# Order of work around three waits of TensorE in a hybrid state-space, attention and expert layer: scores, routing and bias moved

## The chip, the cores and the metric

The kernel runs on one NeuronCore of a Trainium2 chip. The metric is the device time of one execution in microseconds (us), less is better. Engines are named as the profile names them: PE is TensorE (PEld its weight loads, PEq its instruction queue), DVE is VectorE, ACT is ScalarE, POOL is GpSimd, SP is the engine that here only issues transfers. PE works on arrays of SBUF (on-chip memory, 128 partitions) and writes PSUM, eight banks of 512 f32 columns.

## The reference

One layer on 1024 tokens of 1024 channels, all in f32:

```python
h = rmsnorm(x, norm_mix_g); proj = h @ w_in                 # q, k, v (512 each), 8 gates, u (512)
attn = forgetting_attention(q, k, v, log_f)                 # 8 heads of 64
ssm = s5_mixer(u, ...)                                      # 32 groups of 16 channels, state 64
mixed = concatenate([rmsnorm(attn, attn_out_g), rmsnorm(ssm, ssm_out_g)])
x = x + mixed @ w_out
h = rmsnorm(x, norm_ffn_g)
top_val, top_idx = lax.top_k(h @ w_router + b_router, 4)    # of 32 experts
gates = softmax(top_val)
x = x + sum_k gates[k] * (clamped_swiglu(h @ w_gu[e] + b_gu[e]) @ w_dn[e] + b_dn[e])
x = x + ple_in * sigmoid(rmsnorm(x, norm_ple_g) @ w_ple_gate)   # ple_in = p @ w_ple_proj
out = rmsnorm(x, norm_final_g)
```

## The kernel before, in words

Each engine has its own hand-written program, in order; semaphores join them. A wait holds everything that stands behind it on its engine. PSUM banks are dealt out by hand. An f32 matmul is two instructions of PE ("x8" for four of them). The stages in order of time:

1. **Projection and state space (0 to 289 us).** PE computes the 34 units of `PROJ` into banks 2 to 5. Behind every second unit of v, k and q stands a piece of the state-space mixer (`PIECE_AFTER`, `piece`); the last, `piece("out", 3)`, stands behind the last q unit and writes banks 0 and 1, which ACT copies to `u`.
2. **Attention (290 to 417 us).** 32 tiles (a pair of heads, a block of 128 queries). `scores(s)` on PE, `row_low(s)` on DVE, `exp(s)` on ACT, `recip(s)` on DVE, a scaling on POOL, `turn_probs` and `values` on PE. `scores` runs `AHEAD` = 3 tiles ahead, in banks 0 to 3. POOL's loop first waits for the last piece's copy and does the first part of a gelu beside the attention.
3. **Gate of the state-space output (417 to 450 us)**: `wglu` matmuls; DVE and ACT make `ssmT` from them.
4. **Output projection and routing (452 to 602 us).** `project(t, n)` is eight matmuls of 512 columns, four from `attnT`, four from `ssmT`, into banks 0, 1 or 2, 3 in turn. `row_squares` sums squares into banks 4 to 7. DVE (`resid`) adds the result to `x1`, DVE and ACT normalise the block (`norm_rows`, `ffn_norm`), `turn_rows(t)` transposes it, ACT copies it, `route(t)` computes the router's logits, and DVE (`logits`) the four best.
5. **Bias and tables (602 to 656 us).** DVE works out where each (token, expert) row goes: `ohr` and `ohc`, in four parts; ACT scales a part (`tokens_in`), PE multiplies it (L1765), DVE takes `rowid` from the sum, and POOL gathers the first rows of the experts by it. DVE then makes `passtab`, which goes over memory to `passrow`; engines load numbers of passes from it. Beside that, POOL spreads the gates (`gsp`, L575), PE turns them (L1741), and `bias(un)`, un = 0 to 15, adds gate times `b_dn` to `x1`: a matmul of 32 rows (L1754) and an identity matmul that adds `x1` itself (L1755), then a copy by ACT (`bias_out`, L801). SP's first four chunks of the first expert's weights `wg` are issued in this stage, the other four and the four of `wd` once `passrow` and the rows are there.
6. **Experts (656 to 2233 us).** One pass per expert, by number of rows: six narrow passes (L1865, L1887), then wider ones (L1808, L1825). Each pass loads 12 chunks of 1 MB; a chunk's transfer is issued when PE has freed its place.
7. **Tail (2233 to 2397 us)**: `pp` matmuls (L1932), gather of expert rows by POOL, `combine` and `finish` on DVE, gate matmuls (L1948).

## Time and profile before

| | us |
|---|---|
| median of 3 runs | 2413.66 |
| the three runs | 2397.08, 2413.66, 2414.1 |
| the profiled execution | 2398.55 |
| its span, first to last instruction | 2397.0 |
| TensorE clock granted, mean over the span | 0.994 of 2.4 GHz |

Times in the rows below are from the start of the span. In a row of the timeline "xN" counts instructions that the view merged, the number in brackets is idle time of the engine before them and who ended it.

### The profile page before, as it was taken

To read this page: it belongs to the slowest core of one execution; us is meant where nothing else is said; L and a number is where in the kernel's file an instruction comes from. 1 tells how busy PE (TensorE), PEld (TensorE's weight loads), DVE (VectorE), ACT (ScalarE), POOL (GpSimd) and SP (SyncE) were. 2 spreads that over 40 slices of the span, in tenths; PEclk is the share of its full clock that TensorE was granted. 3 is DMA by queue.
4 is the path that set the end of the run, shared out by engine and by line. 5 is a ranking of instruction groups with operands and counts; after the bars stand their busy time and mean duration, and the time that the engine had idled before them with its cause. 6 is when DMAs were issued, how large, how long until landed. Compare 5 with 4: busy or idle time off the path is not lost.

```text
span 2397.0 us, 41448 instructions
## 1 busy us (share of the span) xinstructions
PE 2337.4 (98%) x15586; PEld 1634.8 (68%) x15587; DVE 866.1 (36%) x2024; ACT 468.5 (20%) x940; POOL 444.8 (19%) x713
## 2 busy tenths in 40 slices
PE   8999999899899999999999999999999999999998
PEld 5545466455355577888878878878888887767443
DVE  4544476233543342332323323222322222112374
ACT  3110165311211211111111111111111101110244
POOL 0555587000111111011011110101111000000320
PEclk9999999999999999999999999999999999999999
DMA  5100110201499999989889888867777666542550
GB/s 190 41 23 6 40 37 27 126 36 44 170 383 394 390 403 325 317 312 318 316 317 321 311 317 324 299 246 303 305 310 291 243 230 228 211 167 79 210 176 35
DMA packets 94494, 528.58 MB, mean 221 GB/s; under 512 B 17159, under 2 KB 18199, under 8 KB 42335
## 3 DMA queue, kind: packets, MB, share of 16 engines
q1 hardware_dynamic: 72383, 460.19, 51.5%
q0 software_dynamic: 22048, 67.53, 8.1%
q8 instruction: 42, 0.69, 0.1%
q14 instruction: 21, 0.17, 0.0%
HBM read 495.26 MB, written 31.23 MB: 220 GB/s over the span
## 4 chain that ended last, share of the span: by engine, by line
PE 89%; DVE 4%; issue 3%; ACT 3%; DMA 1%; SPq 0%; POOL 0%; ACTq 0%; DVEq 0%
PE ps L1808 37%; PE ps L1825 15%; PE ps L1865 5%; PE ps L1583 5%; PE ps L1887 3%; PE ps L1688 2%; PE ps L1574 2%; PE ps L1690 2%; PE ps L1842 2%; DVE x L1439 2%; PE ps L1778 1%; PE ps L1602 1%; PE ps L1634 1%; PE ps L1620 1%; PE ps L1669 1%
## 5 line engine op out<-in xcount | busy, mean ns | idle before, releaser
L1808 PEld LDWEIGHTS ps<-xT,wg 128*128 128x128 f32 x6912 | 873.0, 191 | 26.6 <-issue 13.5
L1808 PE MATMUL ps<-xT,wg 128*128 128x128 f32 (+3 forms) x6912 | 889.1, 291 | 0.0
L1430 DVE TENSOR_SCALAR gb<-ps,bcur 128x256 f32<-128x256 f32 x216 | 104.5, 484 | 920.5 <-PE ps L1808 920.5
L1825 PE MATMUL ps<-wd,actT 128*128 128x512 f32 x864 | 375.6, 592 | 0.0
L1825 PEld LDWEIGHTS ps<-wd,actT 128*128 128x128 f32 x864 | 162.1, 190 | 193.7 <-issue 187.3
L893 ACT ACTIVATE sg<-gb 128x256 f32<-128x256 f32 x216 | 90.1, 417 | 785.8 <-DVE gb L1430 785.8
L1865 PE MATMUL ps<-wg,xT 128*32 128x256 f32 x2304 | 131.8, 385 | 3.5 <-issue 3.5
L1948 PE MATMUL ps<-wpg,xnT 128*128 128x512 f32 x256 | 112.9, 595 | 6.2 <-ACT xnT L906 6.2
L843 ACT ACTIVATE yb<-ps 128x512 f32<-128x512 f32 x54 | 31.2, 596 | 402.9 <-PE ps L1825 181.4
L1865 PEld LDWEIGHTS ps<-wg,xT 128*32 128x32 f32 x2304 | 73.8, 111 | 53.0 <-issue 6.7
L610 POOL COPY rowc<-rowid 128x2 uint32 (+1 forms) x34 | 8.8, 260 | 518.5 <-PE ps L1778 490.8
L1420 DVE TENSOR_TENSOR tb<-gb,sg 128x256 f32<-128x256 f32 x216 | 91.9, 426 | 34.8 <-ACT sg L893 34.8
L1431 DVE TENSOR_SCALAR ub<-ps,bcur 128x256 f32<-128x256 f32 x216 | 102.5, 475 | 0.0
L628 POOL DMA_DIRECT2D bin__177<-in_b_exp x33 | 19.0, 576 | 420.2 <-issue 292.5
L1423 DVE SCALAR_TENSOR_TENSOR actT<-ub,tb 128x256 f32<-128x256 f32 x216 | 91.8, 425 | 7.4
L1948 PEld LDWEIGHTS ps<-wpg,xnT 128*128 128x128 f32 x256 | 47.5, 190 | 65.9 <-issue 54.5
L641 POOL DMA_DIRECT2D expert_rows<-yb x48 | 35.1, 741 | 236.4 <-ACT yb L850 163.4
L1887 PE MATMUL ps<-wd,actT 128*32 128x256 f32 x1152 | 64.6, 380 | 3.4 <-ACT actT L869 3.4
L645 POOL DMA_DIRECT2D expert_rows<-yb x60 | 30.0, 501 | 188.0 <-ACT yb L843 181.9
L1688 PE MATMUL ps<-wout,attnT 128*128 128x512 f32 x128 | 59.4, 608 | 5.4 <-issue 2.8
L1401 DVE TENSOR_TENSOR gb<-ps,bb 64x256 f32<-64x256 f32 x36 | 15.0, 417 | 122.7 <-PE ps L1865 122.7
L1439 DVE SCALAR_TENSOR_TENSOR x<-yg,gates,x 128x1024 f32<-128x1024 f32 x32 | 41.1, 1284 | 46.7 <-DMA yg<-expert_rows,slots 45.9
(403 smaller groups left out, 2455.1 us busy)
## 6 DMA issues: line engine op xcount, KB each, us to landing
wg<-in_w_gu SPq DMA_DIRECT2D x264, 1024.0 KB, 7.1
wd<-in_w_dn SPq DMA_DIRECT2D x132, 1024.0 KB, 7.3
expert_rows<-yb POOLq DMA_DIRECT2D x48, 256.0 KB, 8.4
expert_rows<-yb POOLq DMA_DIRECT2D x60, 128.0 KB, 4.4
hT<-in_x_cm SPq DMA_DIRECT2D x8, 512.0 KB, 7.2
cumb<-gate_sums SPq DMA_DIRECT2D x4, 1024.0 KB, 4.6
x<-in_x_tm SPq DMA_DIRECT2D x1, 4096.0 KB, 13.5
wout<-in_w_out SPq DMA_DIRECT2D x1, 4096.0 KB, 20.9
```

What stands on the lines that cost most here:

```text
L893: a.activation(sg[:, f % 2, :], gb[:, f % 2, :], ACT.Sigmoid, scale=1.702).then_inc(S("sig_ready"), 1)
L1420: v.tensor_tensor(tb[:, f % 2, :], gb[:, f % 2, :], sg[:, f % 2, :], ALU.mult).then_inc(S("tb_ready"), 1)
L1423: v.scalar_tensor_tensor(actT[:, f, :], ub[:, f % 2, :], -6.0, tb[:, f % 2, :], ALU.max, ALU.mult).then_inc(S("act_ready"), 1)
L1430: v.tensor_scalar(gb[:, f % 2, :], ps[:, f % 2, 0:W], bcur[:, f:f + 1], 7.0, ALU.add, ALU.min).then_inc(S("g_ready"), 1)
L1431: v.tensor_scalar(ub[:, f % 2, :], ps[:, f % 2, W:2 * W], bcur[:, 8 + f:9 + f], 8.0, ALU.add, ALU.min).then_inc(S("gu_evac"), 1)
L1583: ins = m.matmul(ps[:, bank, :], w_[:, k, un[1] * P:un[1] * P + P], hT[:, k, 512 * un[2]:512 * un[2] + 512], start=(k == 0), stop=(k == KT ...
L1688: m.matmul(ps[:, 2 * (w % 2), :], attnT[:, k, t * P:t * P + P], wout[:, k, n * 512:n * 512 + 512], start=(k == 0), stop=(k == 3))
L1808: ins = m.matmul(ps[:, f % 2, g_ * W:g_ * W + w], wg[:, f, k, g_, :], xT[:, k, 0:w], start=(k == 0), stop=(k == KT - 1))
L1825: ins = m.matmul(ps[:, 2 + c, :], actT[:, f, 0:P], wd[:, c, f, :], start=(f == 0), stop=(f == FT - 1))
L1865: ins = m.matmul(ps[GR * j:GR * j + GR, ut % 2, 0:256], xT[:, k, GR * r:GR * r + GR], wg[:, f0:f0 + 2, k, j // 2, :], start=(k == 0), stop ...
L1887: ins = m.matmul(ps[GR * j:GR * j + GR, 2 + r // 2, 256 * (r % 2):256 * (r % 2) + 256], actT[:, f, GR * r:GR * r + GR], wd[:, j // 2, f, 2 ...
L1948: ins = m.matmul(ps[:, 2 + n, :], xnT[:, t % 2, k, :], wpg[:, k, n * 512:n * 512 + 512], start=(k == 0), stop=(k == KT - 1))
```

## The change

Four things are done; no arithmetic is added or left out except that a quarter of the bias no longer passes through an identity matmul.

- **Scores first.** PE computes `scores(0)` and `scores(1)` right behind the last q unit, then `piece("out", 3)`, which now writes banks 6 and 7. ACT does `exp(0)` ahead of the piece's copy. `scores(0)` waits only for the q units before the last.
- **Projection split.** `attn_part(0, 0)`, `attn_part(0, 1)` stand ahead of the wait for `ssmT`. `row_squares` writes bank 7 alone, so both projections of block 1 stand right behind it, the first in banks 4 and 5. `turn_rows(t)` stands behind `project(t + 1, 1)` and `route(t)` one block later than before.
- **Bias in quarters.** `bias(r, ...)`: four 32-row matmuls in a row, in four different row strips and four banks, then four identity matmuls. Quarters 0 and 1 stand ahead of the table matmuls, quarter 2 behind them, quarter 3 behind the expert passes, in banks 0, 1, 6, 7 and without identity matmuls: DVE adds it to `x1` with two instructions. ACT copies quarters 0 to 2.
- **Work off POOL.** `gsp` is now 32 small ACT instructions (16 for each half of the tokens, the second half between `tokens_in`), the two memsets go to DVE behind `passtab`.
- The first `turn_half` of the experts' rows waits no longer for `passrow`, the second rows and the last bias copy.

```diff
+OUT_BANK = [0] * (NB - 1) + [6]
+WO_BANK = [0, 2, 4] + [2 * (w % 2) for w in range(3, 16)]
...
-            pool.wait_ge(S("rt_evac"), 9)
-            pool.wait_ge(S("sel_ready"), 8)
             pool.wait_ge(S("hs_st"), 16 * 8)
-            g.tensor_tensor(gsp[:, :, :, :], oh[:, :, :, :].rearrange("p t k e -> p k t e"),
-                            gates[:, :, :].rearrange("p t k -> p k t").unsqueeze(3).to_broadcast([P, TOPK, 8, 32]), ALU.mult).then_inc(S("gs_ready"), 1)
-            link(g.memset(yb[:, 1, :], 0.0))
-            g.memset(xT[:, :, P:W], 0.0).then_inc(S("gu_evac"), 2)
...
-            for s in range(AHEAD):
+            exp(0)
+            piece("out", NB - 1)
+            for s in range(1, AHEAD):
                 exp(s)
...
+            act.wait_ge(S("rt_evac"), 9)
+            act.wait_ge(S("hs_st"), 16 * 8)
+
+            def gates_in(half, part):
+                t = 4 * half + part
+                for k in range(TOPK):
+                    ins = a.activation(gsp[:, k, t, :], oh[:, t, k, :], ACT.Copy, scale=gates[:, t, k:k + 1])
+                if part == 3:
+                    ins.then_inc(S("gs_ready"), 1)
...
+            def bias_out(r):
+                for j in range(4):
+                    act.wait_ge(S("wo_mm"), 17 + 4 * r + j)
+                    a.activation(x1[:, 4 * (r // 2) + j, 512 * (r % 2):512 * (r % 2) + 512], ps[:, 2 + j, :], ACT.Copy).then_inc(S("wo_evac"), 1)
...
-            for un in range(6):
-                bias_out(un)
-            tokens_in(0)
-            for q in range(1, 4):
+            for part in range(4):
+                gates_in(0, part)
+            gates_turned(0)
+            bias_out(0)
+            bias_out(1)
+            for q in range(4):
                 tokens_in(q)
-                bias_out(5 + q)
-            for un in range(9, 16):
-                bias_out(un)
+                gates_in(1, q)
+            gates_turned(1)
+            bias_out(2)
...
+            dve.wait_ge(S("hs_st"), 16 * 8)
+            link(v.memset(yb[:, 1, :], 0.0))
+            v.memset(xT[:, :, P:W], 0.0).then_inc(S("gu_evac"), 2)
...
-            dve.wait_ge(S("wo_evac"), 32)
+            dve.wait_ge(S("wo_evac"), 28)
+            dve.wait_ge(S("wo_mm"), 29)
+            v.tensor_tensor(x1[:, 4:6, 512:D], ps[:, 0:2, :], x1[:, 4:6, 512:D], ALU.add)
+            v.tensor_tensor(x1[:, 6:8, 512:D], ps[:, 6:8, :], x1[:, 6:8, 512:D], ALU.add).then_inc(S("wo_evac"), 1)
...
+            pe.wait_ge(S("pj_evac"), len(PROJ) - 2)
+            pe.wait_ge(S("sy_evac"), NB - 1)
+            pe.wait_ge(S("k_evac"), NB)
+            scores(0)
             pe.wait_ge(S("pj_evac"), len(PROJ))
-            pe.wait_ge(S("sy_evac"), NB)
-            for s in range(AHEAD):
+            scores(1)
+            piece("out", NB - 1)
+            for s in range(2, AHEAD):
                 scores(s)
...
             pe.wait_ge(S("an_ready"), 4)
+            pe.wait_ge(S("out_ld"), 48)
+            attn_part(0, 0)
+            attn_part(0, 1)
             pe.wait_ge(S("ssm_ready"), 8)
-            pe.wait_ge(S("out_ld"), 48)
-            project(0, 0)
-            project(0, 1)
+            ssm_part(0, 0)
+            ssm_part(0, 1)
             row_squares()
+            project(1, 0)
+            project(1, 1)
             pe.wait_ge(S("sm_ready"), 1)
-            for t in range(8):
-                if t + 1 < 8:
-                    project(t + 1, 0)
+            turn_rows(0)
+            for t in range(1, 7):
+                project(t + 1, 0)
+                route(t - 1)
+                project(t + 1, 1)
                 turn_rows(t)
-                if t + 1 < 8:
-                    project(t + 1, 1)
-                route(t)
+            route(6)
+            turn_rows(7)
+            route(7)
...
+            def bias(r, banks, alone):
+                i, n = r // 2, r % 2
+                for j in range(4):
+                    ins = m.matmul(ps[:, banks[j], :], gdT[32 * j:32 * j + 32, i, :], bdn[32 * j:32 * j + 32, 512 * n:512 * n + 512],
+                                   start=True, stop=alone, skip_group_check=True)
+                if alone:
+                    ins.then_inc(S("wo_mm"), 1)
+                else:
+                    for j in range(4):
+                        m.matmul(ps[:, banks[j], :], ident, x1[:, 4 * i + j, 512 * n:512 * n + 512], start=False, stop=True,
+                                 skip_group_check=True).then_inc(S("wo_mm"), 1)
+            gates_turn(0)
             pe.wait_ge(S("out_ld"), 112)
...
+            bias(0, (2, 3, 4, 5), False)
+            pe.wait_ge(S("wo_evac"), 20)
+            bias(1, (2, 3, 4, 5), False)
             for q in range(4):
                 pe.wait_ge(S("tok_ready"), 2 * q + 2)
...
+            gates_turn(1)
+            pe.wait_ge(S("wo_evac"), 24)
+            bias(2, (2, 3, 4, 5), False)
...
+            pe.wait_ge(S("rows0_ld"), 16)
+            turn_half(0)
             pe.wait_ge(S("tab_ld"), 16)
-            pe.wait_ge(S("rows0_ld"), 16)
-            pe.wait_ge(S("rows1_ld"), 16)
             n_next = pe.alloc_register("n_rows_next")
             pe.reg_load(n_next, passrow[0:1, 2:3])
-            pe.wait_ge(S("wo_evac"), 32)
-            turn_rows_in(n_next)
+            pe.wait_ge(S("rows1_ld"), 16)
+            pe.wait_ge(S("wo_evac"), 28)
+            turn_second(n_next)
...
+            pe.wait_ge(S("xt_evac"), npass * 2 + 2)
+            bias(3, (0, 1, 6, 7), True)
             pe.wait_ge(S("wpp_ld"), 32)
             pe.wait_ge(S("y_evac"), npass + 1)
             for i in range(16):
+                if i == 2:
+                    pe.wait_ge(S("wo_evac"), 29)
```

**Scores, on PE.** Where stage 1 ends, PE's program was (the last q unit reads `w_q`; `toep` and `xs_r`, `xs_i` are the last state-space piece, `kA,qA` with `mask_qk` are scores):

```order
L1583 MATMUL ps<-hT,w_q 128x512 x16
L1523 MATMUL ps<-toep,ugT 128x128 x8
L1530 MATMUL ps<-ca_r,xs_r 128x128 x8
L1530 MATMUL ps<-ca_i,xs_i 128x128 x8
L1602 MATMUL ps<-kA,qA 128x128 x2
L1606 MATMUL ps<-mask_qk,ident_b 128x128 x2
L1602 MATMUL ps<-kA,qA 128x512 x4
```

and is now:

```order
L1605 MATMUL ps<-hT,w_q 128x512 x16
L1624 MATMUL ps<-kA,qA 128x128 x2
L1628 MATMUL ps<-mask_qk,ident_b 128x128 x2
L1624 MATMUL ps<-kA,qA 128x512 x4
L1628 MATMUL ps<-mask_qk,ident_b 128x128 x2
L1545 MATMUL ps<-toep,ugT 128x128 x8
L1552 MATMUL ps<-ca_r,xs_r 128x128 x8
L1552 MATMUL ps<-ca_i,xs_i 128x128 x8
L1624 MATMUL ps<-kA,qA 128x256 x2
```

The first two tiles' scores stand ahead of the piece, the third's behind it.

**Projection, on PE.** At the start of stage 4 PE's program was (`wout` with `attnT` or `ssmT` is the projection, `ones` the squares, `cst,hn` a block's transposes, `wr` its routing):

```order
L1688 MATMUL ps<-wout,attnT 128x512 x4
L1690 MATMUL ps<-wout,ssmT 128x512 x4
L1688 MATMUL ps<-wout,attnT 128x512 x4
L1690 MATMUL ps<-wout,ssmT 128x512 x4
L1680 MATMUL ps<-ones,sqs 128x128 x8
L1680 MATMUL ps<-ones,sqat 128x128 x8
L1688 MATMUL ps<-wout,attnT 128x512 x4
L1690 MATMUL ps<-wout,ssmT 128x512 x4
L1699 MATMUL ps<-cst,hn 128x128 x8
```

and is now:

```order
L1718 MATMUL ps<-wout,attnT 128x512 x8
L1723 MATMUL ps<-wout,ssmT 128x512 x8
L1710 MATMUL ps<-ones,sqs 128x128 x8
L1710 MATMUL ps<-ones,sqat 128x128 x8
L1718 MATMUL ps<-wout,attnT 128x512 x4
L1723 MATMUL ps<-wout,ssmT 128x512 x4
L1718 MATMUL ps<-wout,attnT 128x512 x4
L1723 MATMUL ps<-wout,ssmT 128x512 x4
L1737 MATMUL ps<-cst,hn 128x128 x8
```

Both `attnT` halves of block 0 stand together and first, and both projections of block 1 stand between the squares and the first transposes.

**Bias, on ACT.** In stage 5, behind the copy of the ranks (`smap`), ACT's program was (`gdT` the turned gates, `x_133` the bias copies into `x1`, `ohc` the tables):

```order
L793 ACTIVATE smap<-ps 128x256
L795 ACTIVATE gdT<-ps 128x256
L801 ACTIVATE x_133<-ps 128x512 x6
L809 ACTIVATE ohc<-ohc,cst 128x432 x4
L801 ACTIVATE x_133<-ps 128x512
L809 ACTIVATE ohc<-ohc,cst 128x432 x2
```

and is now:

```order
L791 ACTIVATE smap<-ps 128x256
L800 ACTIVATE gsp<-oh,gates 128x32 x16
L807 ACTIVATE gdT<-ps 128x128
L813 ACTIVATE x_133<-ps 128x512 x8
L821 ACTIVATE ohc<-ohc,cst 128x432 x2
L800 ACTIVATE gsp<-oh,gates 128x32 x4
L821 ACTIVATE ohc<-ohc,cst 128x432 x2
```

Sixteen spreads of the gates stand ahead of everything else, two more bias copies stand ahead of the first table part, and four spreads behind each table part.

## Rows read from the trace of the kernel before

**Rows 1.** Timeline of projection and routing: start us, us, instruction, [idle before <- who].

```profile
452.48 5.37 PE L1688 MATMUL ps<-wout,attnT 128*128 128x512 f32 x8 [2.82 <-issue]
...
474.34 3.67 PE L1688 MATMUL ps<-wout,attnT 128*128 128x512 f32 x8 [2.62 <-DVE x L1244]
...
505.42 1.95 PE L1709 MATMUL ps<-wr,h2T 128*128 128x128 f32 x16
...
583.96 3.60 PE L1690 MATMUL ps<-wout,ssmT 128*128 128x512 f32 x8
...
592.37 1.42 PE L1699 MATMUL ps<-cst,hn 128*128 128x128 f32 x8 [3.03 <-DVE hn L1253]
...
594.90 3.78 PE L1709 MATMUL ps<-wr,h2T 128*128 128x128 f32 x16 [1.11 <-ACT h2T L784]
...
598.80 0.19 DVE L1257 TENSOR_TENSOR lg<-ps,brt 128x32 f32<-128x32 f32 x1 [4.47 <-PE ps L1709]
```

**Rows 2.** Timeline where attention starts.

```profile
285.27 1.95 PE L1523 MATMUL ps<-toep,ugT 128*128 128x128 f32 x16
...
290.48 0.49 PE L1602 MATMUL ps<-kA,qA 64*128 64x128 f32 x4 [1.28 <-ACT u L693]
...
295.56 0.16 DVE L1168 RECIPROCAL rden<-den 128x2 f32<-128x2 f32 x1
```

**Rows 3.** Timeline at the start of the tail.

```profile
2234.18 27.73 PE L1932 MATMUL ps<-wpp,ppT 128*128 128x512 f32 x64 [1.18 <-ACT yb L845]
```

**Rows 4.** Stretches: us, busy us (instructions) by engine, PE clock granted, DMA share, GB/s.

```profile
586.00:608.00 22.00, 14.25 (x67) 11.37 (x66) 13.28 (x53) 4.66 (x8) 3.81 (x3) 0.77 0.14 48
700.00:840.00 140.00, 137.74 (x2388) 81.42 (x2384) 51.96 (x144) 26.80 (x68) 23.00 (x40) 1.00 1.00 395
```

**Rows 5.** Timeline of the bias and the tables.

```profile
601.58 1.96 POOL L575 TENSOR_TENSOR gsp<-oh,gates 128x1024 f32<-128x1024 f32 x1 [178.03 <-DVE gates L1293]
601.70 0.39 ACT L793 ACTIVATE smap<-ps 128x256 f32<-128x256 f32 x1 [0.88 <-PE ps L1735]
601.73 2.31 DVE L1300 SCALAR_TENSOR_TENSOR rt<-rt 128x32 f32<-128x32 f32 x3
...
603.60 3.49 PE L1741 MATMUL ps<-cst,gsp 128*128 128x128 f32 x16 [1.94 <-POOL gsp L575]
...
607.56 1.12 PE L1754 MATMUL ps<-bdn,gdT 32*128 32x512 f32 x2 [0.47 <-ACT gdT L795]
...
609.67 1.12 PE L1754 MATMUL ps<-bdn,gdT 32*128 32x512 f32 x2
609.77 0.60 ACT L801 ACTIVATE x<-ps 128x512 f32<-128x512 f32 x1 [2.27 <-PE ps L1755]
...
618.23 1.05 DVE L1349 TENSOR_TENSOR ohc<-pcr,cst 128x864 f32<-128x864 f32 x1
...
626.74 1.19 ACT L809 ACTIVATE ohc<-ohc,cst 128x432 f32<-128x432 f32 x2
...
635.88 0.27 DVE L1365 CAST rowid<-ps 128x108 uint32<-128x108 f32 x1 [7.37 <-PE ps L1765]
...
644.59 2.13 SPq L370 DMA_DIRECT2D wg<-in_w_gu  x4
...
651.20 1.09 PE L1778 MATMUL ps<-cst,xg 128*128 128x128 f32 x8 [0.69 <-ACT x L801]
...
655.79 13.24 PE L1865 MATMUL ps<-wg,xT 128*32 128x256 f32 x192 [3.49 <-issue]
```

**Rows 6.** Attention scores of two heads in two row strips, four instructions.

```profile
308.36 1.13 PE L1602 MATMUL ps<-kA,qA 64*128 64x512 f32 x4
```

**Rows 7.** Chain of work that ended last: start us, us (first halves of two narrow passes).

```profile
693.69 10.36 PE ps L1865 x192
...
728.70 10.36 PE ps L1865 x192
```

**Rows 8.** Transfers issued in 646.8:649: count, KB each, median us to landing.

```profile
wd<-in_w_dn SPq DMA_DIRECT2D x4, 1024.0 KB, 20.4
```

More of the change, by code:

```diff
@@ L726, in _ @@
                         a.activation(azf[:, :], azf[:, :], ACT.Ln, bias=1.0).then_inc(S("lf_out"), 1)
-                if i in PIECE_AFTER:
+                if i in PIECE_AFTER and i < len(PROJ) - 1:
                     piece(*PIECE_AFTER[i])
@@ L1585, in _ @@
                 ins.then_inc(S("pj_mm"), 1)
-                if i in PIECE_AFTER:
+                if i in PIECE_AFTER and i < len(PROJ) - 1:
                     piece(*PIECE_AFTER[i])
@@ L1679, in row_squares, with attn_part, ssm_part, project @@
                     sq = sqs[:, 0, c * P:c * P + P] if c < 8 else sqat[:, (c - 8) * P:(c - 7) * P]
-                    ins = m.matmul(ps[:, 4 + c // 4, (c % 4) * P:(c % 4) * P + P], sq, ones[:, :], start=True, stop=True)
+                    ins = m.matmul(ps[:, 7, c:c + P], sq, ones[:, :], start=True, stop=True, skip_group_check=True)
                 ins.then_inc(S("ss_mm"), 1)
-            def project(t, n):
+            def attn_part(t, n):
                 w = 2 * t + n
-                if w >= 2:
+                if w >= 3:
                     pe.wait_ge(S("wo_evac"), w - 1)
                 for k in range(4):
-                    m.matmul(ps[:, 2 * (w % 2), :], attnT[:, k, t * P:t * P + P], wout[:, k, n * 512:n * 512 + 512], start=(k == 0), stop=(k == 3))
+                    m.matmul(ps[:, WO_BANK[w], :], attnT[:, k, t * P:t * P + P], wout[:, k, n * 512:n * 512 + 512], start=(k == 0), stop=(k == 3))
+            def ssm_part(t, n):
+                w = 2 * t + n
                 for k in range(4):
-                    ins = m.matmul(ps[:, 2 * (w % 2) + 1, :], ssmT[:, k, t * P:t * P + P], wout[:, 4 + k, n * 512:n * 512 + 512],
+                    ins = m.matmul(ps[:, WO_BANK[w] + 1, :], ssmT[:, k, t * P:t * P + P], wout[:, 4 + k, n * 512:n * 512 + 512],
                                    start=(k == 0), stop=(k == 3))
                 ins.then_inc(S("wo_mm"), 1)
+            def project(t, n):
+                attn_part(t, n)
+                ssm_part(t, n)
             def turn_rows(t):
                 pe.wait_ge(S("hn_ready"), t + 1)
+                pe.wait_ge(S("wo_evac"), 3)
                 if t:
@@ L1735, in _, with gates_turn @@
             m.matmul(ps[:, 0, 0:256], tri, sel[:, :, :].rearrange("p t e -> p (t e)"), start=False, stop=True, skip_group_check=True).then_inc(S("cnt_mm"), 1)
-            pe.wait_ge(S("gs_ready"), 1)
-            for i in range(2):
+            def gates_turn(half):
+                pe.wait_ge(S("gs_ready"), half + 1)
                 for k in range(TOPK):
-                    ins = m.matmul(ps[:, 7, i * P:i * P + P], gsp[:, k, 4 * i:4 * i + 4, :].rearrange("p t e -> p (t e)"), ident,
+                    ins = m.matmul(ps[:, 7, half * P:half * P + P], gsp[:, k, 4 * half:4 * half + 4, :].rearrange("p t e -> p (t e)"), ident,
@@ L1757, in _ @@
-            for un in range(6):
-                bias(un)
+                ins.then_inc(S("cnt_mm"), 1)
+                pe.wait_ge(S("ht_evac"), 9 + half)
+            def bias(r, banks, alone):
[5 more added lines that the diff above has]
+                    ins.then_inc(S("wo_mm"), 1)
+                else:
+                    for j in range(4):
+                        m.matmul(ps[:, banks[j], :], ident, x1[:, 4 * i + j, 512 * n:512 * n + 512], start=False, stop=True,
+                                 skip_group_check=True).then_inc(S("wo_mm"), 1)
@@ L1766, in _ @@
                                    start=(c == 0), stop=(c == 31), skip_group_check=True)
-                if q < 3:
-                    bias(6 + q)
             ins.then_inc(S("id_mm"), 1)
-            for un in range(9, 16):
-                bias(un)
+            gates_turn(1)
+            pe.wait_ge(S("wo_evac"), 24)
+            bias(2, (2, 3, 4, 5), False)
             def turn_half(a_):
```

38 lines of the change are left out of this document (15 added, 23 removed).

## The prediction, made before the changed kernel was run

> **What bounds the kernel now.** I read the waits of PE first, to see whether anything but PE is worth moving. Apart from the start, while the inputs load, and the tail, its longest waits are about 3 us each, as the three gaps in [rows 1]: PE is the bound almost everywhere, and its order matters only around some ten gaps. Then I read the timeline around each gap and, above all, what hangs on the work behind it. Three places result.
>
> *Attention's start.* The last state-space piece runs from 285.27; PE then waits 1.28 us for ACT's copy and starts the scores at 290.48. The first reciprocal comes at 295.56 [rows 2]; POOL's scaling and PE's transposes hang on it.
>
> *Projection.* PE waits 2.82 us for the last `ssmT`, and the eight instructions behind that wait take 5.37, where eight of the same kind take 3.60 at 583.96 (64 in a row take 27.73 [rows 3], 0.43 each, so eight cost PE 3.4); it waits 2.62 for DVE at 474.34. At the end it waits 3.03, and then the transposes take 1.42 and the routing 3.78, where the same routing took 1.95 at 505.42 [rows 1]. The granted clock from 586 to 608 is 0.77 [rows 4]: part of it ran at 1.2 GHz, behind PE's gaps.
>
> *Tables.* The sixteen bias units come 2.10 us apart (607.56 to 609.67). They are spread between the table parts, which puts `rowid` at 635.88, though DVE had waited 7.37 us for it; and seven of them stand behind the tables. The first expert pass starts at 655.79 [rows 5].
>
> The sum is made against the profiled execution: 2398.55 us, a span of 2397.0 and 1.55 around it. The median shown, 2413.66, is of three runs of which two lie 16 us higher; nothing in the trace tells why.
>
> **Scores.** After the last q unit at 285.3, tile 0's scores take 0.6; tile 1 waits for DVE's last copy (about 0.9 behind), takes 2.3, and the piece starts at 288.5, 3.2 later than before. Its 3.9 us (285.27 to ACT's copy) end at 292.4. By then DVE is done with tiles 0 and 1, whose scores were 5.1 us ahead of the first reciprocal. Only tile 2 is left, about 1.9 (0.9 on PE, 0.9 on DVE, an estimate from the 5.1 for all three), so the reciprocal comes at 294.3 instead of 295.56: **-1.3 us**. ACT's copy for POOL's gelu is 3 us later, but POOL's first work is the scaling behind that same reciprocal. Bounds: 0, if POOL is late through the copy; -3.9, if the whole piece is hidden.
>
> **Projection.** Two `attnT` halves, 6.9 us, fill the wait for `ssmT`: -2.8, and -1.9 since PE has no gap to slow down behind (5.37 against 3.4). The two projections of block 1, 13.7 us, fill the wait behind the squares: -2.6, and -0.2 for a slow restart (3.67). The last block's transposes of block 6 move behind the last projection, where PE waits anyhow: -0.9. In the loop, each block's routing now comes one projection later; DVE's `logits` then stand ahead of the next `resid`, which gets 3.4 us late, and the projection that needs that bank starts 8 us later still: nothing. The last normalisation (4.97 us from the last projection's end to 592.37) stays on the path; ACT's copy of block 6 now comes ahead of it, +0.2. But of its 5 us PE fills 2.7 with block 6, where it filled 1.8, and its longest gap is 1.3 instead of 3.03. I take full speed behind it: transposes -0.4, routing -1.8. Sum: -2.8 - 1.9 - 2.6 - 0.2 - 0.9 + 0.2 - 2.2 = **-10.4 us**; -8.2 if the last routing stays slow.
>
> **Tables.** Let z be DVE's last addition of logits, 598.80 before. Before: `smap` was copied at z + 3.3, `rowid` began at z + 37.1, the first pass at z + 57.0 [rows 5]. Now, on ACT and PE:
> - 16 spreads on ACT. No row has a 128x32 instruction with a scale in a series. Two of 432 columns take 1.19, so 0.55 each; taking off 400 columns at the 0.86 ns of a bias copy's column (0.60 for 512, against 0.39 for 256 at 601.70) leaves 0.21. Bounds 0.1 and 0.3: 16 take 3.4 (1.6 to 4.8), to z + 6.7.
> - PE has waited about 3.9 us by then and will run slow, as behind the 1.94 us wait before (3.49 for 16 instructions, against 1.95 for 16 of that size at 505.42). Eight instructions take 1.8, the copy and the start 0.4: z + 8.9.
> - A quarter: four 32-row matmuls in four strips, then four identity ones. No row has four strips. Two strips at a time took 1.13 for four instructions of 512 columns [rows 6], where one after another they take 1.72. So eight cost between 0.9 (all four side by side) and 3.4 (none); nearest is side by side, and I take 1.2, with 0.2 for the change of shape (2.10 for a unit against 4 x 0.43) and 3.4 for the identities: 4.8. Half of the first quarter at 1.2 GHz adds 2.4. With ACT's last copy, 0.6, two quarters end at z + 8.9 + 7.8 + 0.6 + 5.0 = z + 22.3.
> - DVE has had the first table part at 619.28, z + 20.5, and is now quicker by 2: beside POOL's `gsp` three instructions took 2.31. That is cover, not gain; ACT is later. Each part now takes ACT 1.19 + 4 x 0.21 = 2.04: the fourth is scaled at z + 22.3 + 6.1 + 1.2 = z + 29.6, PE needs 2.0, `rowid` z + 31.6. That is 5.5 sooner.
> - From `rowid` on, before: 8.7 us to SP's next chunk (644.59), which waits for `passrow`, a number and the gathered rows; then PE's seven units, and 4.6 from the first rows' transposes (651.20) to the pass. Now PE does the second gate turn, 1.2, and quarter 2 with its copy, 5.4, inside the 8.7. The transposes wait only for the first rows; behind `passrow` stay the loads of numbers, 4.1 (4.6 less the 0.5 till the first of them). The pass starts at z + 31.6 + 8.7 + 4.1 = z + 44.4: **-12.6 us**.
>
> POOL's memsets on DVE stand behind `passtab`, where DVE is idle till the first pass; ACT needs them 4 us later.
>
> On the four strips the Trainium skill (TensorE: Matmul & The Clock Gate, Part 3, Measured speedup vs the span model) gives 3.07 times for four strips of 32 rows and 512 columns. By it the eight would take an estimated 1.1 instead of 1.2, and the sum would be 0.2 better; without any overlap it would be 5.4 worse. The trace shows two strips only.
>
> **Experts.** Six narrow passes of 35.0 us move 12 MB each with the transfers busy all the time (share 1.00, 395 GB/s [rows 4]; their first halves start 35.0 apart [rows 7]). The first pass used to start 11.2 us behind SP's chunk issue (644.59), now 4.1. Its second half begins 10.4 into it at full speed [rows 7], or 13.2 as before [rows 5]; its four `wg` chunks stand ahead of the four of `wd`, which landed 20.4 us after their issue in the median [rows 8], that is at 668, four apart by 2.5: the last `wg` at about 660 to 662, 15 to 17 behind 644.59. Needed at 4.1 + 10.4 to 13.2 = 14.5 to 17.3. `wd`, all there at about 672 (+27), is needed at 4.1 + 24 to 27. I take 0, bounds 0 and +7.1, the whole lead.
>
> **Tail.** Quarter 3 is four strips, 1.2 us, inside PE's 1.18 us wait [rows 3]; DVE's two additions are done before the third unit: **0** (+0.2 at most).
>
> Sum: -1.3 - 10.4 - 12.6 = **-24.3**; 2398.55 - 24.3 = **2374 us**.
>
> **Rivals.**
> - *The strips don't overlap.* Against it speaks the pair. Two quarters cost 2.2 more each ahead of `rowid`, the third has 2.1 us of room: -24.3 + 4.5 = -19.8, **2379**.
> - *The lead is lost.* The first passes wait for weights up to 7.1 us; for it speaks the share of 1.00: -17.2, **2381**.
> - *The clock stays low through the bias.* Behind a longer gap than before both quarters would run at 1.2 GHz: 4.8 more for the second, 2.4 for the first, -17.1, **2381**. The Trainium skill (same page, Part 1, What's actually happening) states this rule against the change: PE falls to 1.2 GHz when idle and returns only after sustained work. The trace agrees as far as it goes: 1.42 and 3.78 behind a gap of 3.03.
> - *The gains are refilled.* ACT's spreads and four-copy quarters put `rowid` where it was (at 0.3 us a spread, 1.4 more ahead of the quarters and 0.4 in each part, and 3 more of slow clock), 7.1 of the tables' 12.6 are left, and 8.2 of the routing's: -16.6, **2382**.
> - *The level.* The time falls among the two upper runs: 2414 - 24.3, **2389**.
> - *Slower than before.* The narrow passes become bound by transfers, since the lead that hid them is gone: 12.6 million bytes in 35.0 us need 359 GB/s. At 320 a pass takes 39.4, 4.4 more, and six take 26 more; from there the change loses. At 310 it is 34 - 24, **2408**. Against it speaks 395 GB/s over four passes.
>
> **How the numbers follow.** Forecast 0.48, with its own range of 2367 to 2381; strips 0.09, lead 0.12, clock 0.08, refilled 0.05, level 0.15, slower 0.03. 2365 to 2391 leaves out the last and the forecast's ends. Measurements of this kernel can tell about 1%, 24 us, from no change. My forecast lies on that line: a little over half of it counts as faster against a run of the same level, nearly all of it against the median shown; the rivals of 15 to 20 us mostly as the same. Faster 0.56, same 0.41, slower 0.03.
>
> **What would show it.** The scores behind the last q unit without a gap, the first reciprocal 1.3 earlier. No PE gap at either end of the squares; the last routing in 1.95. Four 32-row matmuls in 1.2. `rowid` 5.5 and the first pass 12.6 closer to DVE's last logits. No PE gap in the narrow passes. Wrong would be: a PE gap in front of L1817 (the tables) of over 3 us, waits for `wg` in the first two passes, or the spread taking ACT over 5 us.

## The result, and the profile after

| | before | after |
|---|---|---|
| median of the runs, us | 2413.88 (4 runs, 2397.08 to 2417.89) | 2374.99 (4 runs, 2373.32 to 2376.21) |
| profiled execution, span | 2397.0 | 2372.4 |
| granted TensorE clock, mean | 0.994 | 0.994 |

The ratio of the runs is 0.9839, its 95% interval 0.9812 to 0.9866. The two profiles are 24.6 us apart, the medians 38.9. By the prediction's own line of 1% the change is faster: the whole interval lies below 0.99. Two questions are left: where the 24.6 come from, and what the other 14 are.

Start of the attention in the kernel after, timeline (start us, us, instruction, [idle before <- who]):

```profile
285.67 0.49 PE L1624 MATMUL ps<-kA,qA 64*128 64x128 f32 x4
...
288.56 2.00 PE L1545 MATMUL ps<-toep,ugT 128*128 128x128 f32 x16
...
292.38 0.60 PE L1624 MATMUL ps<-kA,qA 64*128 64x256 f32 x4
...
292.60 1.08 ACT L689 ACTIVATE u<-ps 128x512 f32<-128x512 f32 x2 [4.78 <-PE ps L1552]
...
293.93 0.16 DVE L1181 RECIPROCAL rden<-den 128x2 f32<-128x2 f32 x1
...
298.37 1.65 PE L1624 MATMUL ps<-kA,qA 64*128 64x384 f32 x4 [2.94 <-DVE low L1174]
```

The first reciprocal comes 1.63 us sooner than in [rows 2]. But its line as a whole, in the view of one source line, ends where it did (before: 295.6 to 407.8):

```profile
L1181 DVE RECIPROCAL rden<-den x32: 153/166/167, 293.9 to 407.9; 128x2 f32<-128x2 f32 x32
```

Projection and routing after, timeline; compare [rows 1]:

```profile
449.50 7.03 PE L1718 MATMUL ps<-wout,attnT 128*128 128x512 f32 x16
...
456.37 7.03 PE L1723 MATMUL ps<-wout,ssmT 128*128 128x512 f32 x16
463.23 1.95 PE L1710 MATMUL ps<-ones,sqs 128*128 128x128 f32 x16
465.02 1.95 PE L1710 MATMUL ps<-ones,sqat 128*128 128x128 f32 x16
466.80 3.60 PE L1718 MATMUL ps<-wout,attnT 128*128 128x512 f32 x8
...
584.04 1.09 PE L1737 MATMUL ps<-cst,hn 128*128 128x128 f32 x8 [0.93 <-DVE hn L1266]
...
586.25 2.05 PE L1747 MATMUL ps<-wr,h2T 128*128 128x128 f32 x16 [1.11 <-ACT h2T L782]
...
588.42 0.19 DVE L1270 TENSOR_TENSOR lg<-ps,brt 128x32 f32<-128x32 f32 x1 [2.42 <-PE ps L1747]
```

No gap is left at the `ssmT` wait or at the squares, and the last transposes and the last routing run at full speed. DVE's last addition of logits, z, stands at 588.42 instead of 598.80.

Bias, tables and the first pass after, timeline; compare [rows 5]:

```profile
591.59 3.48 ACT L800 ACTIVATE gsp<-oh,gates 128x32 f32<-128x32 f32 x16
...
595.13 2.07 PE L1786 MATMUL ps<-cst,gsp 128*128 128x128 f32 x8 [3.86 <-ACT gsp L800]
...
597.57 2.09 PE L1797 MATMUL ps<-bdn,gdT 32*128 32x512 f32 x8 [0.37 <-ACT gdT L807]
...
599.59 4.50 PE L1803 MATMUL ps<-x,cst 128*128 128x512 f32 x8
...
604.77 1.14 PE L1797 MATMUL ps<-bdn,gdT 32*128 32x512 f32 x8 [0.69 <-ACT x L813]
...
605.84 3.70 PE L1803 MATMUL ps<-x,cst 128*128 128x512 f32 x8
...
610.07 1.19 ACT L821 ACTIVATE ohc<-ohc,cst 128x432 f32<-128x432 f32 x2
...
611.32 7.87 PE L1817 MATMUL ps<-ohc,ohr 128*128 128x128 f32 x64 [1.77 <-ACT ohc L821]
...
619.29 0.27 DVE L1378 CAST rowid<-ps 128x108 uint32<-128x108 f32 x1 [3.58 <-PE ps L1817]
...
632.14 12.13 PE L1921 MATMUL ps<-wg,xT 128*32 128x256 f32 x192 [5.99 <-issue]
...
644.93 3.66 PE L1921 MATMUL ps<-wg,xT 128*32 128x256 f32 x64 [0.40 <-DMA wg<-in_w_gu]
```

The first quarter begins at 1.2 GHz (strips 2.09, identities 4.50), the second runs at full clock (1.14 and 3.70). The first pass starts at 632.14, 23.65 earlier than in [rows 5]; from the second pass on everything stands 24.30 earlier, and at the end of the span 24.6.

### The profile page after: what moved, and what is told of

Read it like the earlier page. It is cut to its first block, busy times and chain, and to the rows that moved or that the text cites. A ratio compares the mean times of both kernels' runs of the same rounds, so it can differ in the third digit from the quotient of the medians.

```text
span 2372.4 us, 41466 instructions
## 1 busy us (share of the span) xinstructions
PE 2315.8 (98%) x15578; PEld 1628.3 (69%) x15579; DVE 867.6 (37%) x2028; ACT 471.9 (20%) x969; POOL 439.8 (19%) x710
## 4 chain that ended last, share of the span: by engine, by line
PE 90%; DVE 4%; ACT 3%; issue 2%; DMA 1%; SPq 0%; ACTq 0%; DVEq 0%
PE ps L1864 37%; PE ps L1881 16%; PE ps L1921 5%; PE ps L1605 5%; PE ps L1943 3%; PE ps L1596 2%; PE ps L1718 2%; PE ps L1723 2%; PE ps L1898 2%; DVE x L1456 2%; PE ps L1829 1%; PE ps L1624 1%; PE ps L1558 1%; PE ps L1658 1%; PE ps L1698 1%
## 5 line engine op out<-in xcount | busy, mean ns | idle before, releaser
L1723 PE MATMUL ps<-wout,ssmT 128*128 128x512 f32 x128 | 57.4, 592 | 0.0
```

The source lines that it names most:

```text
L1723: ins = m.matmul(ps[:, WO_BANK[w] + 1, :], ssmT[:, k, t * P:t * P + P], wout[:, 4 + k, n * 512:n * 512 + 512], start=(k == 0), stop=(k == 3))
```

## The experiments

Ratios are against the kernel before, run beside the variant, with 95% intervals. Executions of one kernel differ by several us (2373.59 to 2378.63 in the four of passtab_first), and their mean granted clock goes with it (0.995 in the shortest of these, 0.993 in the longest). A term of 1 or 2 us is therefore read from the stretch of the trace that it is about, and not from the median. z is, as in the prediction, the start of DVE's last addition of logits.

**The two levels of the kernel before.** First the kernel before, unchanged.

> The kernel before, unchanged, for the two levels of its time (2397 and 2414 to 2418). Theory A: the level is a property of this kernel's order and shows again in some of its runs, about 17 us apart; if the profiled run is an upper one, one stretch of its trace holds the 17 us (A1: narrow passes wait for weights; A2: PE at 1.2 GHz somewhere). Rival: the level belongs to the chip or the hour and every kernel of this call shows it.

Twelve runs, 2411.64 to 2419.97, median 2416.9 (ratio 1.0014, 0.9997 to 1.0032). Of the 23 runs beside them two stood near 2398; of all 66 runs of this kernel on record five did, between 2397.08 and 2399.08, and none of the others is below 2411. These are called the lower and the upper level. The profiled run was an upper one, span 2414.7. Its timeline, and two stretches of the busy time (us, busy us and count of PE, PEld, DVE, ACT and POOL, then granted clock, DMA share, GB/s):

```profile
610.00 2.07 PE L1754 MATMUL ps<-bdn,gdT 32*128 32x512 f32 x2 [0.47 <-ACT gdT L795]
612.00 2.08 PE L1755 MATMUL ps<-x,cst 128*128 128x512 f32 x2
...
632.03 2.08 PE L1755 MATMUL ps<-x,cst 128*128 128x512 f32 x2
635.88 3.78 PE L1765 MATMUL ps<-ohc,ohr 128*128 128x128 f32 x16 [1.77 <-ACT ohc L809]
...
646.09 1.12 PE L1754 MATMUL ps<-bdn,gdT 32*128 32x512 f32 x2
...
654.05 0.27 DVE L1365 CAST rowid<-ps 128x108 uint32<-128x108 f32 x1 [23.39 <-PE ps L1765]
```

```profile
604.00:644.00 40.00, 36.02 (x63) 14.84 (x64) 25.48 (x60) 6.66 (x13) 3.53 (x3) 0.50 0.26 105
645.00:665.00 20.00, 20.00 (x72) 9.28 (x71) 6.19 (x18) 5.54 (x10) 3.70 (x6) 1.00 0.23 69
```

The same stretch of the profile before, in the same view:

```profile
604.00:644.00 40.00, 37.75 (x132) 18.25 (x131) 29.59 (x76) 11.90 (x21) 3.79 (x5) 0.97 0.34 132
```

The upper level is TensorE at 1.2 GHz through the bias units: a pair takes 2.07 instead of 1.12, a unit 4.0 instead of 2.1, `rowid` comes at 654.05, and the span is 17.7 longer. Not all of that is the bias: z stands at 600.95, 2.15 later than in [rows 1], and `rowid` 53.10 behind z instead of 37.08, which is 16.0. Theory A2 holds, A1 falls. From 610.00 to 634.1 PE had no gap at all, and the clock did not rise. The two profiles part just ahead of the bias: both turn the gates at 1.2 GHz at first, but in the profile before the clock rose within the turn (granted 0.64 from 605.5 to 607.1, then 1.00, and the first unit at full clock), in the upper run it did not (0.50 from 605.7 to 612).

**One part put back, three kernels.** Each is the kernel after with the whole code of before in one part, on all engines; a line or two of each on PE, in the order scores, projection, bias:

```diff
-            scores(0)
+            pe.wait_ge(S("sy_evac"), NB)
...
-                project(t + 1, 0)
-                route(t - 1)
-                project(t + 1, 1)
+                if t + 1 < 8:
+                    project(t + 1, 0)
                 turn_rows(t)
...
+                if t + 1 < 8:
+                    project(t + 1, 1)
+                route(t)
...
-            bias(0, (2, 3, 4, 5), False)
+            for un in range(6):
+                bias(un)
```

> The kernel after, with the start of attention as before. Theory: the 1.6 us by which the first reciprocal came earlier are gone by the fifth tile (305.59 against 305.68), so this part is worth nothing: the span stays within 0.4 of 2372.4, first reciprocal near 295.6, last again near 407.8. Rival, the prediction's term: 1.3 to 1.6 us longer, about 2374.

Measured: span 2372.1, four runs from 2373.39 to 2375.66 (ratio 0.9842, 0.9801 to 0.9883): the same as the kernel after. First reciprocal 295.7, last 407.9. The other traces bear it out: with the scores as before the last reciprocal stands between 407.70 and 409.63 (four traces), with the scores first between 407.17 and 408.60 (seven). The first part of the change is worth nothing that stands out of this scatter.

> The kernel after, with projection and routing in the order of before. Theory, the prediction's term: 10.4 us longer, span about 2382.8, DVE's last addition of logits near 598.8, what follows moved as one. Rival: part of it is hidden in the tables, which wait for nothing of TensorE that early: less than 8.

Measured: span 2382.4, 10.0 more; z at 598.82, 10.40 more. Median 2384.69 (ratio 0.9886, 0.9844 to 0.9927). The forecast's term; the rival falls. The 10.4 hold where the last routing runs at full clock, as it does in eight of the ten traces with the new order; in the other two (alternate and two, below) it took 3.64 and 3.68 instead of 2.05 and z came some 2 us later.

> The kernel after, with bias, tables and start of the experts as before. Theory: 13.9 us longer up to the second pass and 0.3 in the tail, span about 2386.6. Rival, the prediction's term: 12.6. For the level: if this kernel shows runs 17 us above its lowest and the other two do not, the level belongs to the way into the passes; if undo_projection shows them, to the routing.

Ten runs: three from 2386.97 to 2391.62, seven from 2400.22 to 2404.69; median 2402.32 (ratio 0.9937, 0.9912 to 0.9961). Lowest against lowest it is 13.65 more than the kernel after, but the three lower runs are spread over 4.7 us, so they can't tell the prediction's 12.6 from the theory's 14.2. The profiled run was an upper one, with z at 588.57, as in the kernel after, and the clock of the bias at half:

```profile
596.00:630.00 34.00, 31.76 (x45) 10.81 (x45) 21.36 (x49) 6.14 (x11) 0.00 (x0) 0.50 0.30 124
```

So the level belongs to the order of the bias. The other two undone kernels show no second level in four runs each, nor do the 36 runs in all of kernels whose bias is in quarters.

**Does the clock alone make it?** The kernel before with filler for TensorE in two waits.

```diff
+            def warm(n):
+                for _ in range(n):
+                    m.matmul(ps[:, 6, 0:P], ident, ident, start=True, stop=True, skip_group_check=True)
+            warm(6)
             pe.wait_ge(S("cs_ready"), 8)
...
+            warm(8)
             pe.wait_ge(S("gs_ready"), 1)
```

> The kernel before, with matmuls of the identity by itself into an idle bank in TensorE's two waits behind the routing (6 and 8 of 128 columns, about 1.4 and 1.9 us at full clock, no more than the waits of 1.6 and 1.9); nothing else changes. Theory: the upper level is TensorE staying at 1.2 GHz through the bias units (604 to 645 in the upper trace), and it falls in that state because of the waits ahead of them. Filled, the clock is high when the bias begins, no run is an upper one, and the median is 2394 to 2398 instead of 2415. Rival: the 32-row matmuls themselves bring the clock down, the filler changes nothing, and the runs lie at 2412 to 2420.

Four runs, 2396.03 to 2400.28, median 2398.34, against 2414.39 of the kernel before beside it (ratio 0.9926, 0.9907 to 0.9945). Its timeline, and its stretch of the bias:

```profile
605.16 1.95 PE L1731 MATMUL ps<-cst 128*128 128x128 f32 x16
607.27 2.05 PE L1747 MATMUL ps<-cst,gsp 128*128 128x128 f32 x16 [0.16 <-POOL gsp L575]
609.79 1.12 PE L1760 MATMUL ps<-bdn,gdT 32*128 32x512 f32 x2 [0.47 <-ACT gdT L795]
```

```profile
603.00:640.00 37.00, 34.31 (x151) 18.85 (x149) 29.45 (x81) 10.82 (x20) 5.09 (x5) 1.00 0.28 114
```

Fourteen matmuls that compute nothing take 16 us off the kernel before: all four runs are lower ones, where five of 66 are without them. In this trace z came late (602.47), but `rowid`, at 638.11, only 35.64 behind it. The theory holds.

**Which trait of the quarters ends the level?** The same matmuls in another order.

```diff
                     ins = m.matmul(ps[:, banks[j], :], gdT[...], bdn[...], start=True, stop=alone, skip_group_check=True)
+                    if not alone:
+                        m.matmul(ps[:, banks[j], :], ident, x1[...], start=False, stop=True,
+                                 skip_group_check=True).then_inc(S("wo_mm"), 1)
                 if alone:
                     ins.then_inc(S("wo_mm"), 1)
-                else:
-                    for j in range(4):
-                        m.matmul(ps[:, banks[j], :], ident, x1[...], start=False, stop=True,
-                                 skip_group_check=True).then_inc(S("wo_mm"), 1)
```

> The kernel after, but in quarters 0 to 2 each 32-row matmul is followed at once by its identity matmul, as in the kernel before; the same matmuls in another order. Theory: it is this alternation that keeps TensorE at 1.2 GHz once it is there, since in the upper runs it had no gap for 25 us and the clock stayed low, while four identities in a row behind four strips bring it back (at 601.23 in the kernel after). So here the bias begins at 1.2 GHz as in the kernel after, a quarter takes 16.4 us (4 units of 4.1) instead of 4.8 to 6.5, rowid comes 20 to 23 us later and the span is near 2393 to 2396 in most runs; a few may escape. Rival: only the strips' overlap is lost, a quarter takes 8.4, rowid comes 6 to 8 us later, span 2378.5 to 2380.5 in all runs.

Ten runs, all from 2397.76 to 2402.58, median 2399.17 (ratio 0.9946, 0.9927 to 0.9966); span 2398.0. Its timeline:

```profile
590.58 0.19 DVE L1270 TENSOR_TENSOR lg<-ps,brt 128x32 f32<-128x32 f32 x1 [4.00 <-PE ps L1747]
...
597.29 2.08 PE L1786 MATMUL ps<-cst,gsp 128*128 128x128 f32 x8 [3.85 <-ACT gsp L800]
599.73 2.07 PE L1797 MATMUL ps<-bdn,gdT 32*128 32x512 f32 x2 [0.37 <-ACT gdT L807]
601.73 2.08 PE L1800 MATMUL ps<-x,cst 128*128 128x512 f32 x2
...
630.53 2.08 PE L1800 MATMUL ps<-x,cst 128*128 128x512 f32 x2
634.38 9.11 PE L1816 MATMUL ps<-ohc,ohr 128*128 128x128 f32 x64 [1.77 <-ACT ohc L821]
...
643.59 0.27 DVE L1378 CAST rowid<-ps 128x108 uint32<-128x108 f32 x1 [25.73 <-PE ps L1816]
```

`rowid` comes at 643.59, 24.3 later than in the kernel after, and the first pass at 658.61. But 2.16 of the 24.3 are there already at z, since the last routing ran at 1.2 GHz in this run; from z on it is 22.1, within the 20 to 23 of the theory. The span, 2398.0, lies 2 over the theory's range for that reason and because the first pass starts 15.0 behind `rowid` instead of 12.85. Side by side:

| run (profiled execution) | z | `rowid` behind z | clock of the bias units |
|---|---|---|---|
| before | 598.80 | 37.08 | full |
| before_warm | 602.47 | 35.64 | full |
| before_again | 600.95 | 53.10 | half up to 644 |
| undo_bias | 588.57 | 52.28 | half |
| alternate | 590.58 | 53.01 | half up to 634 |
| after | 588.42 | 30.87 | half, then full from 601 |

With the pairs alternating again the way from z to `rowid` is as long as in the upper run of before: all that the quarters gain there hangs on four strips and four identities each standing together. In the medians that is 24 of the 39 us. Lost overlap of the strips alone, the rival, would have cost 6 to 8. All ten runs are upper ones; where five of 66 escape in the kernel before, ten can't tell whether fewer do here. The run undoes two things at once, the four strips side by side and the four identities in a row; which of them brings the clock back is not tested.

**Why the scores gave nothing.** The piece is moved behind the third tile's scores.

```diff
-            exp(0)
-            piece("out", NB - 1)
-            for s in range(1, AHEAD):
+            for s in range(AHEAD):
                 exp(s)
+            piece("out", NB - 1)
...
             scores(1)
+            scores(2)
             piece("out", NB - 1)
-            for s in range(2, AHEAD):
-                scores(s)
...
-            pool.wait_ge(S("sy_evac"), NB)
...
+                if s == 1:
+                    pool.wait_ge(S("sy_evac"), NB)
+                    gelu_in(0)
```

> The kernel after, with the last state-space piece behind the scores of all three first tiles, its copy behind the exponentials of all three, and POOL's first gelu behind the second scaling. Theory: in the kernel after the gain of the scores was lost since the third tile's scores stand behind the piece and the second tile's exponential behind its copy, and the longer wait of TensorE (2.94) brought the clock down for twice as long. Here the first reciprocal comes 2.5 to 3.2 us sooner, at 290.8 to 291.4, TensorE's wait shrinks below 1.5, and 2 to 3 us are left at the last reciprocal: span 2369.5 to 2370.5. Rival: the attention is bound by POOL or the exponentials from the second tile on; the last reciprocal stays at 407.9 and the span at 2372.4.

Measured: span 2370.3, median 2372.01 (ratio 0.9822, 0.9803 to 0.9840). Its timeline, and the reciprocals' line:

```profile
289.66 2.00 PE L1546 MATMUL ps<-toep,ugT 128*128 128x128 f32 x16
...
293.49 1.67 PE L1625 MATMUL ps<-kA,qA 64*128 64x512 f32 x8
...
295.93 0.92 PE L1625 MATMUL ps<-kA,qA 64*128 64x384 f32 x4 [0.33 <-DVE low L1175]
```

```profile
L1182 DVE RECIPROCAL rden<-den x32: 151/166/168, 290.8 to 406.2; 128x2 f32<-128x2 f32 x32
```

The first reciprocal is 3.1 earlier than in the kernel after, TensorE's wait of 2.94 has become 0.33, and 1.7 are left at the last reciprocal, 2.1 at the end. The span fits the theory; the 1.7 lie under its 2 to 3. That it is no scatter three traces show: with this order the last reciprocal stands at 406.18 here, 406.42 and 404.81 in the two combined kernels below, and at 407.17 or later in all others.

**The clock at the start of the quarters.** The kernel after with `warm(6)` and `warm(14)` in the same two waits as in before_warm.

> The kernel after, with 6 and 14 such matmuls in the same two waits (1.6 and 3.9 us). Theory: gate turn 2.07, strips 2.09 and identities 4.50 fall to 1.06, 1.14 and 3.70, 2.8 us, and the tables wait for that bias copy, so rowid comes 2.8 sooner and the span is 2369.6. Rival 1: DVE's table parts hide it, rowid gains under 1, span 2371.5 to 2372.4. Rival 2: the filler itself runs at 1.2 GHz (the routing's gaps of 1.1 have already brought the clock down), takes twice as long and delays the gate turn: span 2373 to 2376.

Measured: span 2370.3, median 2372.31 (ratio 0.9822, 0.9803 to 0.9840). Timeline:

```profile
595.68 1.16 PE L1791 MATMUL ps<-cst,gsp 128*128 128x128 f32 x8 [0.73 <-ACT gsp L800]
...
597.21 1.14 PE L1802 MATMUL ps<-bdn,gdT 32*128 32x512 f32 x8 [0.37 <-ACT gdT L807]
598.28 3.70 PE L1808 MATMUL ps<-x,cst 128*128 128x512 f32 x8
```

Turn, strips and identities take 1.16, 1.14 and 3.70 as expected; z came 0.55 later in this run (the last reciprocal too, by 0.7), from z on `rowid` is 2.65 sooner, for the 2.8 of the theory. The span is 2.1 less, 0.7 above the forecast.

**The way into the first pass.** In the kernel after DVE stood idle for 3.58 us ahead of `rowid`, with `passtab` still to make.

```diff
-            dve.wait_ge(S("id_mm"), 1)
-            v.tensor_copy(rowid[:, :], ps[:, 1, P - nh:P]).then_inc(S("rowid_ready"), 1)
...
             v.tensor_copy(passtab[:, :], tabf[:, :]).then_inc(S("tab_ready"), 1)
+            dve.wait_ge(S("id_mm"), 1)
+            v.tensor_copy(rowid[:, :], ps[:, 1, P - nh:P]).then_inc(S("rowid_ready"), 1)
```

> The kernel after, with DVE's work for passtab (2.5 us) ahead of its wait for the table matmuls, in which it stood idle for 3.58 us. Theory: the way into the first pass goes over passtab, passrow and the loads of numbers, not over the gathered rows: passtab 3.1 us sooner (at 618.6), the first pass 2 to 3 us sooner, span 2369.5 to 2370.5. Rival: the first pass waits for rows or weights: span 2372.0 to 2372.6, with waits for wg in the first passes.

A miss: span 2374.8, 2.4 longer; median 2375.86 (ratio 0.9836, 0.9816 to 0.9856), no better than the kernel after. Timeline:

```profile
618.16 0.92 SPq L384 DMA_DIRECT2D passrow<-passtab  x1
...
622.80 0.64 POOL L584 DMA_DIRECT2D bin__177<-in_b_exp  x1
...
629.16 2.10 SPq L374 DMA_DIRECT2D wg<-in_w_gu  x4
...
633.53 6.65 PE L1921 MATMUL ps<-wg,xT 128*32 128x256 f32 x72 [7.45 <-issue]
```

`passrow` goes out 3.8 sooner, but that lets POOL issue its bias loads at 622.80 instead of 628.95, and the second rows, issued at the same time as before (621.76 against 621.84), land 7.2 behind their issue instead of 5.2, at 628.96 instead of some 627.1. SP's chunks, ACT and PE all wait for them. Neither theory had that. That accounts for the 1.4 by which the pass starts later. The other 1.0 of the 2.4 is clock: the pass's first half took 13.12, for 12.13 in the kernel after, and since it takes 13.36 and 13.38 in undo_scores and piece_late, which leave this stage alone, that part is scatter.

```diff
-            for f in range(4):
+            for f in range(FT):
                 gu_chunk(e0, f)
...
+            pool.wait_ge(S("rows1_ld"), 16)
             pool.dma_start(bin_[:, :], ...)
...
+            ends = [pe.value_load(...) for c in range(NW)]
             pe.wait_ge(S("rows1_ld"), 16)
```

> The kernel after, with four edits on the way into the first pass: all eight wg chunks of the first expert issued in one go (four more at about 600 instead of 627.85), passtab ahead of rowid on DVE, POOL's loads of the input bias behind the landing of the second rows, TensorE's loads of pass bounds ahead of its wait for those rows. Theory: in passtab_first the second gather landed 1.9 us later (628.95 against 627.06) since POOL's bias loads, freed early, ran beside it, and SP, ACT and TensorE all wait for it; and the first pass's second half waits for wg, issued behind it. With both out of the way the first pass starts at 629.5 to 630.3 instead of 632.14, has no wait for wg, and the span is 1.8 to 2.5 less, 2370. Rival 1: eight chunks in a row are still under way at 620 and hold up the gathers: rows at 627 or later, span 2372 to 2374. Rival 2: the rest of the numbers' loads, not the second rows, bounds the start: span 2371.5 to 2372.5.

With passtab first and these three edits (the lines that they replace are left out here): span 2371.1, median 2372.57 (ratio 0.9830, 0.9813 to 0.9846). The second rows land at 627.1 again, the first pass starts at 630.03, 2.11 sooner, and its second half waits for nothing. But its first half took 13.12 again, the scatter just named, so 1.6 are left at the second half (643.35), 1.2 at the second pass (667.98) and 1.3 at the end. The start fits the theory, the gain is 0.5 below its range. Rival 1 falls: eight chunks in a row did not hold up the rows. That POOL's loads had done so rests on this one run, which changes the chunks and the loads of numbers too.

**Together.** `two` is piece_late and warm_routing, `four` has the edits of entry too, and ten filler matmuls ahead of the first pass.

> The kernel after, with the edits of piece_late and warm_routing together, 2.0 and 2.05 us less each alone. Theory: they lie on different stretches and add, span 2368.0 to 2368.8. Rival: the first pass's second half waits for wg, whose chunks move with rowid, so nothing is lost either, but the clock in the attention takes 0.7 back as in warm_routing: 2369 to 2370.

> The edits of two and of entry together, and ten matmuls of the identity between TensorE's loads of pass bounds, so that the first pass does not begin at 1.2 GHz. Theory: 2368.4 less 2 for the entry, less about 1.5 for the clock of the first 3 us of the pass: span 2365 to 2366.5. Rival: rowid comes at 615, the last chunks are under way till 619 and hold up the gathers by 1 to 3 us: 2367 to 2369.

`two`: median 2369.26, runs 2368.84 to 2371.44 (ratio 0.9817, 0.9801 to 0.9834). Its profiled run, 2369.9, is the slowest of the four and lies in the rival's range, though not for the rival's reason: there the last routing ran at 1.2 GHz, z at 588.47 though the last reciprocal stood at 406.42. The other three runs are 1.8 to 2.6 shorter, near the theory. `four`: median 2369.65, runs 2367.55 to 2371.87 (ratio 0.9822, 0.9806 to 0.9839). Its profiled run is its fastest, span 2366.0, and the only one of this case with the full clock all the way:

```profile
285.00:660.00 375.00, 354.97 (x2492) 214.32 (x2494) 194.00 (x570) 145.96 (x327) 113.00 (x136) 1.00 0.28 107
```

That run met the theory; its other runs, 2 to 4 us longer, don't (two of them lie in the rival's range), and no trace shows them. All runs of both are below the kernel after (2373.32 at best), which was measured at another time; which of the two is better stays open.

## Why the prediction was right, and where it was not

The forecast was 2374, range 2365 to 2391; measured 2374.99. The sum said 24.3 us between the profiled executions; it was 24.6. Four of its terms were off, and they cancelled: the scores gave 1.3 less than forecast, tables, experts and tail together 1.6 more. That is luck, of a size within the scatter of single runs. A larger piece of luck is that the median itself came to the forecast. The sum started from a lower run of the kernel before, which few of its runs are; it holds for the median because the change takes the upper level away, which nothing in the sum foresaw.

- **Scores, forecast -1.3: 0.** The first reciprocal came 1.63 earlier, as forecast and a little more. The step that failed is taking that reciprocal for the whole stage. The second tile's exponential stands behind ACT's copy of the piece and the fourth tile's scores behind the piece, so 0.75 were left at the second reciprocal (295.97 against 296.72). Then TensorE's wait ahead of the fifth tile's scores grew from 1.91 to 2.94, the clock was low for longer (granted 0.68 and 0.50 from 296 to 300 and 300 to 304, before 0.93 and 0.64), and 0.09 were left at the fifth (305.59 against 305.68). undo_scores shows the zero, piece_late the reason. The bound of 0 was in the text for another reason, POOL.
- **Projection, forecast -10.4: -10.4.** z moved by 10.38, and by 10.40 in undo_projection. The parts fit too: the squares start 4.75 sooner (forecast 4.7), the last normalisation takes 5.13 for 4.97 (0.2 more), the last transposes took 1.09 and the routing 2.05, at full clock, as assumed.
- **Tables, forecast -12.6: -13.3.** The spreads took 3.48 (forecast 3.4), the gate turn was slow (2.07 against 1.8), the strips took 1.14 (1.2) and a quarter at full clock 4.8 (4.8). The size that was off is the slow clock in the first quarter, 1.8 where 2.4 was taken, and the parts, 1.94 apart instead of 2.04. `rowid` came at z + 30.9 (31.6), the pass 12.85 behind it (12.8).
- **Experts, forecast 0: -0.65.** The first half of the first pass took 12.13 for 13.24, with some 3.4 us of it at 1.2 GHz instead of 5.5. Of the lost lead 0.40 us showed, as one wait for `wg`. The prediction had named waits for `wg` in the first two passes as a sign of being wrong; one came, of 0.40, and the rival of 7.1 fell. The later narrow passes keep their 35.0 us.
- **Tail, forecast 0: -0.3.** Quarter 3 takes 1.14 ahead of the `pp` matmuls, inside the wait; the 0.3 came between their start and the transposes behind them (27.58 for 27.92), and why stays open.
- **The level, given 0.15.** The text took the upper runs for a property of the measurement ("nothing in the trace tells why"), to which the kernel after would be as subject as the one before. It is a property of the bias units: with the clock down where they begin, their order keeps it down. The quarters end it, which is worth some 14 to 18 us more against most runs of the kernel before (38.9 less 24.6 in the medians, 17.7 between the two profiles). The rival on the clock through the bias had the right mechanism and applied it only to the kernel after, where it came back while the first quarter's identities ran (granted 0.53 from 594 to 601, 0.99 from 601 to 611).

On the strips, the eight instructions took 1.14 where 0.43 each would be 3.44, 3.0 times. The Trainium skill (TensorE: Matmul & The Clock Gate, Part 3, Measured speedup vs the span model) has 3.07, and the trace agrees. On their price without overlap the prediction has two figures, 5.4 and, among the rivals, 4.5; the 4.5 is the one that its rows give (twice 2.2 and 0.1).

## What to carry to other kernels

When the runs of a kernel have two levels, take the profile of one of each before anything is costed: here the difference between them was larger than any one term of the change, and 14 matmuls that compute nothing removed it. When a stage's first step comes earlier, follow the gain to the stage's last step, past what the moved work now stands in front of. A transfer that is released earlier can delay the one that everybody waits for. And a gain of 1 or 2 us is looked for in its own stretch, since the clock alone moved other stretches by as much from run to run.

## What the runs showed of the hardware

- TensorE stayed at 1.2 GHz from 610.00 to 634.1 without any gap between its instructions, while 32-row and 128-row matmuls of 512 columns alternated (granted clock 0.50 from 604 to 644). The same alternation, begun at 2.4 GHz, stayed there (1.00 from 603 to 640 in before_warm). Four strips side by side and four identities brought it back within 7 us in the kernel after. The Trainium skill (TensorE: Matmul & The Clock Gate, Part 1, What's actually happening) ties the clock to the engine being busy or idle; in the upper runs it was busy by the trace and still slow. Matmuls of 128 rows and 128 columns in a row lifted it too: in before_again (granted 0.50 up to 644.8, 1.00 from 646) and in alternate (0.51 from 636 to 638, 1.00 from 638) the clock rose while the tables ran. What tells the orders apart inside the chip no run here shows.
- ACT did 16 instructions of 128x32 with a scale in 3.48 us, 0.22 apart.
- With three small loads by POOL (8 KB and twice 128 KB) issued in the 2 us behind a gather of 128 rows, the gather landed 1.9 us later; with eight 1 MB chunks issued 20 us ahead of it and the small loads behind it, it did not.
